# A decode step with paged and windowed attention: state values loaded by place, last pages in two partition halves

## The chip, the cores and the metric

The kernel runs on one core of one Trainium2 chip. The metric is the device time of one execution in microseconds; of several executions the median is given.

## The reference, cut to what matters

One layer of a decoder serves 512 prompt tokens and 8 sequences of 8 sample tokens. Half of the heads use differential attention over 4096 cached positions (paged), the other half a dilated window attention over a state of 2048 positions for each sequence. The part that the change touches is the second half for the samples:

```python
def _dilated_attention_sample(q, k_new, v_new, k_buf, v_buf):
    k_all = concatenate([k_buf, k_new], axis=1)      # 2048 + 8 positions
    v_all = concatenate([v_buf, v_new], axis=1)
    for window, d in ((128, 1), (512, 4), (2048, 16)):
        idx = (w + arange(t))[:, None] - d * arange(window // d + 1)[None, :]
        kg, vg = k_all[:, idx], v_all[:, idx]
        ... softmax over the keys, weighted sum of the values
    # the three branches are combined by their denominators
```

Then follow the output projection, a SwiGLU feed-forward and norms. The state shifted by eight positions is an output too.

## The kernel before

The kernel is written out by hand for each engine, with semaphores. All of the samples' attention runs in a loop of 53 slots `t` with eight steps `i` each, between the pieces of the prompt's work (`pieces(t, i)`). A slot handles a *page set* `q` of one item. An item is a pair of sequences; items 0 to 3 are the paged cache (8 sets each of four pages of 128 positions for each sequence), items 4 to 7 the window state (3 sets each). In all there are 44 sets (`KSLOTS`). Slot `t` scores the keys of set `t` and weighs the values of set `t - 8` (`LAG`). So the state's values are weighed in slots 40 to 51.

A state's 2048 positions are seen as `(p i)` with `i = 16`: 128 places `p`, each of 16 positions. The dilation of 16 makes only positions `4g` to `4g + 3` of every place needed for sets g = 0 and 1, and of the last 32 places positions 8 to 15 (set g = 2, `pages_of(q) == 2`). The latter are the two-page sets 34, 37, 40 and 43, weighed in slots 42, 45, 48 and 51. In each set `h` says which sequence of the pair it is.

Keys go into `k_ring` (eight pages of 128 partitions x 512 floats), are turned in 32x32 blocks by DVE (L2153) into `kt_sb`, and TensorE makes scores from them (L1232). Four-page state keys are loaded two pages at a time. A two-page key load has its source turned by `src.rearrange("p j c -> j p c")` from `[32, 4, 512]` to `[4, 32, 512]`, with the destination `k_ring[:, i, :]`, `[128, 512]`.

Values rotate over three buffers (`ring_of`): `v_ring` up to slot 43, then in turn `k_ring` (44, 47, 50), `v_ring` (45, 48, 51) and `t_ring` (46, 49), which lies over `kt_sb`. All two-page sets are in `v_ring`. `place_values` (L666) issues a load of one page of one `h` (256 KB): row `4j + k` of a buffer gets place or position j of page k, in four blocks b. For a two-page set only partitions 0 to 63 are used, each load goes to 32 of them, 8 KB in each, and sequence h lies in half h of the buffer. `weigh_values` waits for all of a half's pages and multiplies: `turn_probs` has turned the probabilities with four transposes (L1245), ACT copied them to `pt_sb` (L1693), and 32 products (L1270) accumulate in `O`, after which `pv_half[h]` counts up. After an item's last set the new rows are weighed (L1283, `pv_items`).

Up to slot 44 SP issues all values' loads, in `load_values(t, h)`, each with a wait that its buffer is free. From slot 47 on ACT issues the half h = 1, after the copy at L1693 of two slots before. On SP the order at the end is: (41, 6) slot 42 half 0; (42, 0) half 1; (42, 6) and (43, 0) slot 43; (43, 1) slot 44 half 0; (43, 4) slot 46 half 0 and slot 44 half 1; (43, 6) slot 45 half 0; (44, 0) slot 46 half 1 and slot 45 half 1; (44, 6), (45, 6), (46, 6), (47, 6), (48, 6) half 0 of slots 47 to 51. The first weights of the feed-forward stage (`g_raw`, 1 MB each, L737) go out between them. The keys of slot t + 2 and t + 1 are issued in the same loop (L768). After the loop SP waits for `pv_items`, loads `x` again (L714) and enters the feed-forward stage, where TensorE works through to the end.

Of the kernel before, what the change touches and what calls it, by code (L numbers as in the profile page):

```python
# [15 lines left out]
P = 128  # L16
# [82 lines left out]
KSLOTS = sum(QUADS)  # L99
# [12 lines left out]
def pages_of(q):  # L112
    it, g = item_of(q)
    return 2 if it >= 4 and g == 2 else 4
# [14 lines left out]

def col0(it, g):  # L130
    return 512 * g + (0 if it < 4 else WCOLS * ((it - 4) % 3))


def mini0(it):
# [155 lines left out]
def landings():  # L290


    seen, k_lands, v_lands = [[0] * 8 for ring in range(3)], {}, {}
    for q in range(KSLOTS):
        for i in range(8):
            if i % 4 < pages_of(q):
                seen[0][i] += key_load(q, i) == i
                k_lands[q, i] = 16 * seen[0][i]
    for q in range(KSLOTS):
        for i in range(8):  # L300
            if i % 4 < pages_of(q):
                here = seen[ring_of(q + LAG)]
                here[i] += 1
                v_lands[q, i] = 16 * here[i]
    return k_lands, v_lands
# [56 lines left out]
def build(nc, ins, outs):  # L362
    from contextlib import ExitStack
    ctx = ExitStack()
    with ctx:
# [291 lines left out]
        def place_values(queue, q, i, src):  # L657


            h, k = divmod(i, 4)  # L660
            n = pages_of(q)
            if n == 4:
                src = src.rearrange("(b j) c -> j b c", b=4)
            rows, ring = slice(k, 32 * n, n), ring_of(q + LAG)
            dst = (k_ring[rows, 4 * h:4 * h + 4, :], v_ring[rows, h, :, :], t_ring[rows, h, :, :])[ring]
            queue.dma_start(dst, src).then_inc((k_landed, v_landed, t_landed)[ring][i], 16)  # L666

        def state_rows(state, q, i):

# [16 lines left out]
        def _(sp):  # L686
# [61 lines left out]
            def load_page(keys, q, i):  # L748

                it, g = item_of(q)  # L750
                h, k = divmod(i, 4)
                n = pages_of(q)
                if it < 4:
                    if k == 0 and g % 2 == 0:
                        first = (2 * it + h) * NPAGES + 4 * g
                        ids[keys, h] = nc.values_load_multi_w_load_instructions(
                            page_ids[0:1, first:first + 8], engines=[sp.engine], min_val=0, max_val=NPOOL - 1,
                            skip_runtime_bounds_check_because="page_table holds numbers of pages in the pool")[1]
                    src = (ck if keys else cv)[ds(ids[keys, h][4 * (g % 2) + k], 1)].squeeze(0)
                else:  # L760
                    src = state_rows(sk if keys else sv, q, i)
                if keys:
                    if n == 2:
                        src = src.rearrange("p j c -> j p c")
                    elif it >= 4:
                        src = state_pair(sk, q, i)
                    at_first = i - (it >= 4 and n == 4)
                    sp.dma_start(k_ring[:, at_first:i + 1, :].squeeze(1) if at_first == i else k_ring[:, at_first:i + 1, :], src)\  # L768
                        .then_inc(k_landed[i], 16)
                else:  # L770
                    place_values(sp, q, i, src)

            def load_keys(t, i):

# [5 lines left out]

            def load_values(t, h):

                if t == KSLOTS:
                    sp.wait_ge(kt_done, half_end(KSLOTS - 1, h))
                elif t == KSLOTS + 1:
                    sp.wait_ge(pv_half[h], t - LAG - 1)
                elif t == KSLOTS + 2:
                    sp.wait_ge(scored if h else half_scored, KSLOTS)
                elif t > KSLOTS + 2:
                    sp.wait_ge(pv_half[h], t - LAG - 2)  # L790
                elif t > LAG:
                    sp.wait_ge(pv_half[h], t - LAG)
                for k in range(pages_of(t - LAG)):
                    load_page(False, t - LAG, 4 * h + k)

            sp.wait_ge(const_in, 16 * N_CONST)
            for i in range(8):
# [73 lines left out]
            for t in range(SLOTS):  # L871
                for i in range(8):
                    if i < 4:
                        load_keys(t + 1, i + 4)
                    else:
                        load_keys(t + 2, i - 4)
                    for p in pieces(t, i):
                        main(p)
                    if i == 0 and has_v(t - 1) and t < KSLOTS:
                        load_values(t, 1)  # L880
                    if i == 6 and has_v(t) and t + 1 < KSLOTS:
                        load_values(t + 1, 0)
                    if (t, i) == (KSLOTS - 1, 1):
                        load_values(KSLOTS, 0)
                    if (t, i) == (KSLOTS - 1, 4):
                        load_values(KSLOTS + 2, 0)
                        load_values(KSLOTS, 1)
                    if (t, i) == (KSLOTS - 1, 6):
                        load_values(KSLOTS + 1, 0)
                    if (t, i) == (KSLOTS, 0):  # L890
                        load_values(KSLOTS + 2, 1)
                        load_values(KSLOTS + 1, 1)
                    if i == 6 and t >= KSLOTS and has_v(t + 3):
                        load_values(t + 3, 0)
                        if not has_v(t + 4):
                            load_pair(1, 1, 0, w_up, True)
                    if (t, i) == (KSLOTS + 1, 1):
                        sp.wait_ge(e_t, KT)
                        load_pair(0, 0, 0, w_gate, True)
# [109 lines left out]
        def _(pe):  # L1009
# [226 lines left out]
            def turn_probs(t):  # L1236

                it, g = item_of(t - LAG)
                n = pages_of(t - LAG)
                pe.wait_ge(exp_done, EXP_NO[it, 4 * half_of(it, g) + 3] + 1)  # L1240
                if X_NO["p", t]:
                    pe.wait_ge(x_free, X_NO["p", t])
                for k in range(4):
                    c = col0(it, g) + 32 * n * k
                    last = nc.tensor.transpose(X[0:32 * n, k * P:(k + 1) * P], s_sb[:, c:c + 32 * n], ident[:, :])  # L1245
                last.then_inc(x_full, 1)

            def turn_new_probs(t):
# [6 lines left out]
            def weigh_values(t, h):  # L1255

                q = t - LAG
                it, g = item_of(q)
                rows = 32 * pages_of(q)
                pe.wait_ge(x_free, X_NO["p", t] + 1)  # L1260
                if g == 0 and h == 0 and it:
                    pe.wait_ge(o_scaled, it)
                ring = ring_of(t)
                landed = (k_landed, v_landed, t_landed)[ring]
                for k in range(pages_of(q)):
                    pe.wait_ge(landed[4 * h + k], V_LANDS[q, 4 * h + k])
                for b in range(4):
                    values = (k_ring[0:rows, 4 * h + b, :], v_ring[0:rows, h, b, :], t_ring[0:rows, h, b, :])[ring]
                    for f in range(4):
                        last = nc.tensor.matmul(O[32 * f:32 * f + 32, P * h:P * h + P], pt_sb[0:rows, 4 * f + b, :],  # L1270
                                                values[:, f * P:(f + 1) * P],
                                                start=g == 0 and b == 0 and h == 0, stop=False, skip_group_check=True)
                last.then_inc(pv_half[h], 1)

            def weigh_new_values(t):
# [2 lines left out]
                s = it // 4  # L1278
                pe.wait_ge(x_free, X_NO["m", t] + 1)
                pe.wait_ge(y_free, Y_NO["g", 2 * s + 1] + 1)  # L1280
                for h in range(2):
                    for f in range(4):
                        last = nc.tensor.matmul(O[32 * f:32 * f + 32, P * h:P * h + P], ptm[:, 32 * f:32 * f + 32],  # L1283
# [183 lines left out]
        def _(act):  # L1467
# [218 lines left out]
            def evac_probs(t):  # L1686
# [2 lines left out]
                act.wait_ge(x_full, X_NO["p", t] + 1)  # L1689
                if q:  # L1690
                    act.wait_ge(pv_half[1], q)
                r = slice(0, 32 * pages_of(q))
                nc.scalar.activation(pt_sb[r].rearrange("p m (k t) -> p k m t", k=4),  # L1693
                                     X[r].rearrange("p (k m t) -> p k m t", k=4, t=DT), ACT.Copy).then_inc(x_free, 1)
                if t > KSLOTS and has_v(t + 2):
                    for k in range(pages_of(q + 2)):
                        place_values(act, q + 2, 4 + k, state_rows(sv, q + 2, 4 + k))

            def evac_new_probs(t):

# [6 lines left out]
            def exps(it, c):  # L1707
# [7 lines left out]
                else:  # L1715
                    bias = bias4[it % 2][:, k:k + 1]
                    if it >= 4 and half:
                        at0 = col0(it, 2) + 64 * k
                        part = s_sb[:, at0:at0 + 64]
                    else:  # L1720
                        at0, n = col0(it, 4 * half), 4 if it < 4 else 2
# [246 lines left out]
        def _(dve):  # L1968
# [209 lines left out]
            def keep_scores(t):  # L2178
# [7 lines left out]
                    dve.wait_ge(lw_in, 16)  # L2186
                mask = lw[:, P * g:P * g + 32 * n] if it >= 4 else zero.to_broadcast([P, 32 * n])
                for k in range(4):
                    c = col0(it, g) + 32 * n * k
# [437 lines left out]
```

## Time and profile before

| | |
|---|---|
| median of 3 runs | 1122.25 us (1115.1 to 1124.65) |
| the profiled execution's own time | 1113.92 us |
| its span | 1112.1 us |
| TensorE busy | 969.6 us, 87% |
| VectorE busy | 668.9 us, 60% |
| ScalarE busy | 505.7 us, 45% |
| DMA queue of SP, share of 16 engines | 80.3% |
| the stretch of the state's values | from 572 us (first issue) to 696 us (last product) |

Times of the trace are from the span's start. A group of instructions is given with its first start and the time that it took. In brackets stands how long the engine had been idle before it and what ended that. The DMA share is the mean busy share of the core's 16 DMA engines; it can come out a little over 1.

### The profile page before, as it was taken

What the parts mean: (1) busy time and instruction counts of PE and PEld (TensorE: products, weight loads), DVE (VectorE), ACT (ScalarE), POOL (GpSimd) and SP (SyncE); (2) the same over time, 40 slices, a digit from 0 to 9 for tenths busy, and PEclk for the clock granted to TensorE, in tenths of its full rate; (3) what the DMA queues carried; (4) which work ended last, traced back from release to release, by engine and by line L of the source; (5) the groups of instructions that cost most, each with busy time, mean ns of one, the idle gap of its engine ahead of it and who ended that gap; (6) DMA issues with size and microseconds to landing.
All of it is one profiled execution on the core that took longest, in us unless ns stands there. A gap on an engine that the chain in (4) does not pass through costs nothing.

```text
span 1112.1 us, 29337 instructions
## 1 busy us (share of the span) xinstructions
PE 969.6 (87%) x11050; PEld 858.7 (77%) x11050; DVE 668.9 (60%) x1627; ACT 505.7 (45%) x1116; POOL 133.9 (12%) x69
## 2 busy tenths in 40 slices
PE   3989898998887779887889667899999999999995
PEld 3978787777764557676667554699999999999994
DVE  5389645675458887754346445788888888700003
ACT  5654543374125656645234262455555555611123
POOL 1322111111000010002111000000000000133330
PEclk8999999999988999888899787899999999999997
DMA  8699999999999999888979798386768686974632
GB/s 249 248 314 346 320 328 344 358 340 334 317 340 338 337 365 329 301 273 293 327 245 298 221 255 223 123 302 264 301 263 301 263 301 252 325 248 159 228 128 85
DMA packets 174933, 310.98 MB, mean 280 GB/s; under 512 B 13601, under 2 KB 87714, under 8 KB 173282
## 3 DMA queue, kind: packets, MB, share of 16 engines
q1 hardware_dynamic: 172898, 305.24, 80.3%
q10 hardware_dynamic: 1920, 4.20, 1.4%
q8 instruction: 74, 1.21, 0.4%
q14 instruction: 41, 0.34, 0.1%
HBM read 302.30 MB, written 73.92 MB: 338 GB/s over the span
## 4 chain that ended last, share of the span: by engine, by line
PE 32%; issue 30%; DMA 11%; SPq 11%; DVE 7%; ACT 7%; ACTq 0%; POOL 0%; DVEq 0%; POOLq 0%
PE ps L1383 11%; DMA v_ring<-in_cache_v_diff 6%; SPq L666 5%; PE ps L1038 5%; PE ps L1270 4%; PE ps L1232 4%; SPq L768 4%; DVE kt_sb L2153 2%; ACT q_st L1678 2%; PE ps L1189 2%; DMA k_ring<-in_state_v_win 2%; DMA k_ring<-in_cache_k_diff 2%; PE ps L1115 1%; DMA v_ring<-in_state_v_win 1%; ACT s_sb L1723 1%
## 5 line engine op out<-in xcount | busy, mean ns | idle before, releaser
L2153 DVE STREAM_TRANSPOSE kt_sb<-k_ring 128x512 f32<-128x512 f32 x336 | 220.5, 691 | 86.5 <-DMA k_ring<-in_cache_k_diff 37.4
L1270 PE MATMUL ps<-v_ring,pt_sb 128*32 128x128 f32 (+1 forms) x2496 | 98.8, 306 | 62.1 <-DMA v_ring<-in_cache_v_diff 49.3
L1270 PEld LDWEIGHTS ps<-v_ring,pt_sb 128*32 128x32 f32 (+1 forms) x2496 | 75.7, 121 | 78.1 <-issue 67.8
L1038 PE MATMUL ps<-h_hi,w_hi 128*128 128x288 f32 x384 | 124.4, 324 | 1.9 <-DVE h_lo L2006 1.9
L1038 PE MATMUL ps<-h_lo,w_hi 128*128 128x288 f32 x384 | 115.0, 299 | 0.0
L1038 PE MATMUL ps<-h_hi,w_lo 128*128 128x288 f32 x384 | 114.7, 299 | 0.0
L1232 PE MATMUL ps<-kt_sb,q_st 128*32 128x128 f32 (+1 forms) x2816 | 97.0, 281 | 10.2 <-DVE q_st L2163 4.6
L989 POOL TENSOR_TENSOR c_lo<-c_raw,c_hi 128x1408 fp32r<-128x1408 f32 x14 | 46.6, 3332 | 440.2 <-ACT c_hi L1781 440.2
L1232 PEld LDWEIGHTS ps<-kt_sb,q_st 128*32 128x32 f32 x2816 | 72.9, 114 | 28.2 <-issue 19.9
L1038 PEld LDWEIGHTS ps<-h_hi,w_hi 128*128 128x128 f32 x384 | 74.0, 193 | 16.1 <-issue 13.8
L949 POOL TENSOR_TENSOR w_lo<-w_raw,w_hi 128x1024 fp32r<-128x1024 f32 x24 | 57.3, 2390 | 229.5 <-ACT w_hi L1492 229.5
L1693 ACT ACTIVATE pt_sb<-ps 128x512 f32<-128x512 f32 (+1 forms) x44 | 26.2, 594 | 129.2 <-PE ps L1245 129.2
L1320 PE MATMUL ps<-t_h,s_h 128*128 128x288 f32 x264 | 77.9, 295 | 1.2 <-ACT u L1774 1.2
L1320 PE MATMUL ps<-t_l,s_h 128*128 128x288 f32 x264 | 77.9, 295 | 0.0
L1320 PE MATMUL ps<-t_h,s_l 128*128 128x288 f32 x264 | 77.7, 294 | 0.0
L2444 DVE TENSOR_TENSOR x<-x,ps 128x512 f32 (+1 forms) x8 | 5.5, 689 | 119.5 <-PE ps L1396 119.5
L2292 DVE TENSOR_TENSOR s_l<-s_t,s_h 128x512 fp32r<-128x512 f32 x88 | 58.8, 689 | 28.4 <-ACT s_h L1745 18.1
L1383 PE MATMUL ps<-a_hi,c_hi 128*128 128x288 f32 x352 | 75.4, 296 | 0.2 <-POOL c_lo L989 0.2
L1383 PE MATMUL ps<-a_lo,c_hi 128*128 128x288 f32 x352 | 75.3, 295 | 0.0
L1383 PE MATMUL ps<-a_hi,c_lo 128*128 128x288 f32 x352 | 74.9, 294 | 0.0
L1038 PEld LDWEIGHTS ps<-h_lo,w_hi 128*128 128x128 f32 x384 | 74.3, 194 | 0.0
L1038 PEld LDWEIGHTS ps<-h_hi,w_lo 128*128 128x128 f32 x384 | 73.9, 192 | 0.0
(236 smaller groups left out, 2289.4 us busy)
## 6 DMA issues: line engine op xcount, KB each, us to landing
k_ring<-in_cache_k_diff SPq DMA_DIRECT2D x256, 256.0 KB, 5.5
v_ring<-in_cache_v_diff SPq DMA_DIRECT2D x256, 256.0 KB, 5.5
out_k_win_sample<-in_state_k_win SPq DMA_DIRECT2D x32, 1020.0 KB, 8.3
out_v_win_sample<-in_state_v_win SPq DMA_DIRECT2D x32, 1020.0 KB, 8.5
k_ring<-in_state_k_win SPq DMA_DIRECT2D x32, 512.0 KB, 7.7
w_raw<-in_w_in SPq DMA_DIRECT2D x24, 512.0 KB, 6.3
g_raw<-in_w_gate SPq DMA_DIRECT2D x11, 1024.0 KB, 5.2
g_raw<-in_w_up SPq DMA_DIRECT2D x11, 1024.0 KB, 5.2
```

Of the source, the lines that this page charges most:

```text
L666: queue.dma_start(dst, src).then_inc((k_landed, v_landed, t_landed)[ring][i], 16)
L768: sp.dma_start(k_ring[:, at_first:i + 1, :].squeeze(1) if at_first == i else k_ring[:, at_first:i + 1, :], src)\
L949: nc.gpsimd.tensor_tensor(w_lo[:, n % 3, :], w_raw[:, n % 3, :], w_hi[:, n % 2, :].bitcast(F32), ALU.subtract).then_inc(w_lo_done, 1)
L989: nc.gpsimd.tensor_tensor(c_lo[j][:, 0:width], c_raw[:, j, 0:width], c_hi[j][:, 0:width].bitcast(F32), ALU.subtract).then_inc(w_lo_done, 1)
L1038: last = nc.tensor.matmul(M[c][:, 0:HALF], wt, act[:, k, c * HALF:(c + 1) * HALF], start=k == 0 and at_first, stop=k == KT - 1 and act is ...
L1232: last = nc.tensor.matmul(S[32 * f:32 * f + 32, c0:c0 + 32 * n], q_st[:, h, f, r, :], kt_sb[:, 4 * h:4 * h + n, c:c + 32], start=r % 2 == ...
L1270: last = nc.tensor.matmul(O[32 * f:32 * f + 32, P * h:P * h + P], pt_sb[0:rows, 4 * f + b, :], values[:, f * P:(f + 1) * P], start=g == 0 ...
L1320: last = nc.tensor.matmul(ps[:, bank, 0:HALF], wt[:, k, :], act[:, k, :], start=j in (0, 1, 3) and k == 0 and at_first, stop=k == 3 and wt ...
L1383: last = nc.tensor.matmul(main_ps[:, 2 * bank + c, 0:HALF], wt[j][:, w], a_lo[:, pair, block, :] if low else a_hi[pair][:, block, :], star ...
L1693: nc.scalar.activation(pt_sb[r].rearrange("p m (k t) -> p k m t", k=4), X[r].rearrange("p (k m t) -> p k m t", k=4, t=DT), ACT.Copy).then_ ...
L2153: V.transpose(kt_sb[:, i, :], k_ring[:, i, :]).then_inc(kt_done, 1)
L2292: V.tensor_tensor(dst[:, :, :], src, high[:, :, :].bitcast(F32), ALU.subtract).then_inc(form_low, 1)
```

## The change

Values of the state are now loaded by `place_state`. For a four-page set a load fills one block b (all 128 partitions, 2 KB in each) from 32 places, and in each place from four positions that lie side by side (8 KB). For a two-page set one load fetches 4 of the 8 positions of both sequences (512 KB), to every second partition of all 128, 8 KB in each; sequence h is now in partitions 64h to 64h + 63, and the set fills only half `it % 2` of `v_ring`. There are two such loads for a set instead of four. The scores of such a set lie in another order (`part0`), are turned with two transposes instead of four and copied with two copies of 64 partitions. TensorE waits block by block in four-page state sets, waits for its own products of h = 0 before those of h = 1 in two-page sets, and for all of them before the new rows of items 4 to 7. Both loads for slot 45 go out at (43, 6); those for slot 48 at (44, 0) and for slot 51 at (45, 6), earlier than before. Slot 43's loads both wait for slot 42's second half.

```diff
+def part0(q, k):
+    it, g = item_of(q)
+    return col0(it, g) + (P * k if pages_of(q) == 4 else 64 * (2 * (k % 2) + k // 2))
@@ landings
-            if i % 4 < pages_of(q):
+            if pages_of(q) == 4 or i - 4 * (item_of(q)[0] % 2) in (0, 1):
@@ place_values: only for n == 4 now, and
+        def place_state(queue, q, h, x):
+            it, g = item_of(q)
+            b, ring = 2 * (it - 4) + h, ring_of(q + LAG)
+            if pages_of(q) == 4:
+                dst = (k_ring[:, 4 * h + x, :], v_ring[:, h, x, :], t_ring[:, h, x, :])[ring]
+                queue.dma_start(dst, sv[b, 32 * x:32 * x + 32, 4 * g:4 * g + 4, :])\
+                    .then_inc((k_landed, v_landed, t_landed)[ring][4 * h + x], 16)
+            else:
+                src = sv[b:b + 2, 96:P, 8 + 4 * x:12 + 4 * x, :].rearrange("h j b c -> h j (b c)")
+                queue.dma_start(v_ring[x:P:2, it % 2, :, :].rearrange("p b c -> p (b c)"), src).then_inc(v_landed[4 * (it % 2) + x], 16)
@@ load_values
+                q = t - LAG
+                if pages_of(q) == 2:
+                    if h == 0:
+                        half = item_of(q)[0] % 2
+                        q0 = {FIRST[4] + 2: q - 1, FIRST[5] + 2: q - 2, FIRST[6] + 2: q - 5, FIRST[7] + 2: q - 6}[q]
+                        sp.wait_ge(pv_half[half], q0 + 1)
+                        for x in range(2):
+                            place_state(sp, q, h, x)
+                    return
-                    sp.wait_ge(pv_half[h], t - LAG)
+                    sp.wait_ge(pv_half[1 if pages_of(q - 1) == 2 else h], q)
@@ SP's loop
                         load_values(KSLOTS + 2, 1)
-                        load_values(KSLOTS + 1, 1)
+                        load_values(KSLOTS + 4, 0)
+                    if (t, i) == (KSLOTS + 1, 6):
+                        load_values(KSLOTS + 7, 0)
                     if i == 6 and t >= KSLOTS and has_v(t + 3):
-                        load_values(t + 3, 0)
+                        if pages_of(t + 3 - LAG) == 4:
+                            load_values(t + 3, 0)
@@ turn_probs
-                for k in range(4):
-                    c = col0(it, g) + 32 * n * k
-                    last = nc.tensor.transpose(X[0:32 * n, k * P:(k + 1) * P], s_sb[:, c:c + 32 * n], ident[:, :])
+                for k in range(n):
+                    c = col0(it, g) + P * k
+                    last = nc.tensor.transpose(X[:, k * P:(k + 1) * P], s_sb[:, c:c + P], ident[:, :])
@@ weigh_values
+                rows, at = (slice(0, P), h) if n == 4 else (slice(64 * h, 64 * h + 64), it % 2)
+                if n == 2 and h == 1:
+                    pe.wait_ge(pv_half[0], q + 1)
+                by_place = it >= 4 and n == 4
                 for b in range(4):
+                    if by_place:
+                        pe.wait_ge(landed[4 * h + b], V_LANDS[q, 4 * h + b])
@@ weigh_new_values
+                if it >= 4:
+                    pe.wait_ge(pv_half[1], FIRST[it] + QUADS[it])
@@ evac_probs
+                    for h in range(2):
+                        r = slice(64 * h, 64 * h + 64)
+                        last = nc.scalar.activation(into[r, 2 * h:2 * h + 2],
+                                                    X[r, 0:2 * P].rearrange("p (k m t) -> p k m t", k=2, t=DT), ACT.Copy)
-                    for k in range(pages_of(q + 2)):
-                        place_values(act, q + 2, 4 + k, state_rows(sv, q + 2, 4 + k))
+                    if pages_of(q + 2) == 4:
+                        for b in range(4):
+                            place_state(act, q + 2, 1, b)
```

## Rows read from the trace of the kernel before

**Rows 1.** The page: busy time of TensorE, and the DMA queue of SP.
```profile
PE 969.6 (87%) x11050; PEld 858.7 (77%) x11050; DVE 668.9 (60%) x1627; ACT 505.7 (45%) x1116; POOL 133.9 (12%) x69
...
q1 hardware_dynamic: 172898, 305.24, 80.3%
```

**Rows 2.** Windows: length, busy times (instructions) of each engine, clock, DMA share, GB/s.
```profile
594.00:595.00 1.00, 1.00 (x23) 0.76 (x13) 0.21 (x1) 1.00 (x2) 0.28 (x1) 1.00 0.96 391
...
600.00:602.00 2.00, 1.29 (x19) 0.95 (x21) 1.97 (x6) 1.91 (x8) 0.00 (x0) 1.00 1.03 382
...
635.00:640.00 5.00, 0.78 (x12) 0.42 (x4) 1.64 (x11) 3.53 (x12) 0.00 (x0) 0.98 1.03 361
640.00:645.00 5.00, 0.20 (x4) 0.20 (x8) 1.60 (x3) 4.94 (x16) 0.00 (x0) 0.50 1.04 224
...
660.00:670.00 10.00, 5.11 (x112) 3.90 (x104) 5.04 (x8) 5.39 (x8) 0.00 (x0) 1.00 1.05 225
...
680.00:690.00 10.00, 6.74 (x139) 5.00 (x137) 3.65 (x7) 1.55 (x2) 0.00 (x0) 0.88 1.01 208
```

**Rows 3.** TensorE in order of time: start, us, line, operation, count, idle before.
```profile
572.04 0.60 PE L1245 MATMUL ps<-ident,s_sb 128*128 128x128 f32 x4
...
620.52 1.93 PE L1270 MATMUL ps<-v_ring,pt_sb 64*32 64x128 f32 x32 [4.82 <-DMA v_ring<-in_state_v_win]
...
622.73 1.94 PE L1232 MATMUL ps<-kt_sb,q_st 128*32 128x128 f32 x32
625.04 1.93 PE L1270 MATMUL ps<-v_ring,pt_sb 64*32 64x128 f32 x32 [0.37 <-DMA v_ring<-in_state_v_win]
...
633.50 0.65 PE L1232 MATMUL ps<-kt_sb,q_st 128*32 128x64 f32 x32
...
644.80 3.64 PE L1270 MATMUL ps<-k_ring,pt_sb 128*32 128x128 f32 x64 [9.02 <-ACT pt_sb L1693]
...
670.14 1.66 PE L1270 MATMUL ps<-v_ring,pt_sb 64*32 64x128 f32 x32 [3.56 <-DMA v_ring<-in_state_v_win]
...
687.42 1.86 PE L1270 MATMUL ps<-k_ring,pt_sb 128*32 128x128 f32 x32 [2.44 <-DMA k_ring<-in_state_v_win]
...
693.16 1.93 PE L1270 MATMUL ps<-v_ring,pt_sb 64*32 64x128 f32 x32
694.87 1.08 PE L1283 MATMUL ps<-v_s,ptm 64*32 64x128 f32 x16
```

**Rows 4.** The chain that ended last: start, us, what.
```profile
612.62 12.28 DMA v_ring<-in_state_v_win
...
668.57 18.71 DMA k_ring<-in_state_v_win
```

**Rows 5.** Windows as in rows 2, of two gaps.
```profile
617.00:620.00 3.00, 0.00 (x0) 0.00 (x0) 1.51 (x6) 0.00 (x0) 0.00 (x0) 0.88 0.25 83
...
575.00:577.00 2.00, 0.00 (x0) 0.00 (x0) 1.20 (x6) 0.00 (x0) 0.00 (x0) 1.00 0.30 101
```

**Rows 6.** SP in order of time: start, us of issuing, line, what, count.
```profile
601.56 3.88 SPq L768 DMA_DIRECT2D k_ring<-in_state_k_win  x4
607.29 1.16 SPq L666 DMA_DIRECT2D v_ring<-in_state_v_win  x2
611.47 0.58 SPq L768 DMA_DIRECT2D k_ring<-in_state_k_win  x1
612.10 1.13 SPq L666 DMA_DIRECT2D v_ring<-in_state_v_win  x2
613.27 0.58 SPq L768 DMA_DIRECT2D k_ring<-in_state_k_win  x1
...
696.01 0.47 SPq L714 DMA_DIRECT2D x<-in_x_sample  x1
```

**Rows 7.** Single durations: ACT's copies, and ACT's issues of loads (ns min/median/max).
```profile
L1693 ACT ACTIVATE pt_sb<-ps x44: 573/597/603, 132.7 to 690.3; 128x512 f32<-128x512 f32 x40, 64x512 f32<-64x512 f32 x4
...
L666 ACTq DMA_DIRECT2D v_ring<-in_state_v_win x4: 509/568/612, 657.9 to 676.5; - x4
```

More of the change, by code:

```diff
@@ L660, in place_values @@
             h, k = divmod(i, 4)
[L661 to L664, printed above, removed]
+            rows, ring = slice(k, P, 4), ring_of(q + LAG)
             dst = (k_ring[rows, 4 * h:4 * h + 4, :], v_ring[rows, h, :, :], t_ring[rows, h, :, :])[ring]
-            queue.dma_start(dst, src).then_inc((k_landed, v_landed, t_landed)[ring][i], 16)
+            queue.dma_start(dst, src.rearrange("(b j) c -> j b c", b=4))\
+                .then_inc((k_landed, v_landed, t_landed)[ring][i], 16)
+        def place_state(queue, q, h, x):
[8 more added lines that the diff above has]
+                queue.dma_start(v_ring[x:P:2, it % 2, :, :].rearrange("p b c -> p (b c)"), src).then_inc(v_landed[4 * (it % 2) + x], 16)
         def state_rows(state, q, i):
@@ L759, in load_page @@
                     src = (ck if keys else cv)[ds(ids[keys, h][4 * (g % 2) + k], 1)].squeeze(0)
-                else:
-                    src = state_rows(sk if keys else sv, q, i)
+                elif keys:
+                    src = state_rows(sk, q, i)
                 if keys:
@@ L769, in load_page @@
                         .then_inc(k_landed[i], 16)
+                elif it < 4:
+                    place_values(sp, q, i, src)
                 else:
-                    place_values(sp, q, i, src)
+                    place_state(sp, q, h, k)
             def load_keys(t, i):
@@ L781, in load_values @@
             def load_values(t, h):
+                q = t - LAG
[7 more added lines that the diff above has]
+                    return
                 if t == KSLOTS:
                     sp.wait_ge(kt_done, half_end(KSLOTS - 1, h))
-                elif t == KSLOTS + 1:
-                    sp.wait_ge(pv_half[h], t - LAG - 1)
                 elif t == KSLOTS + 2:
@@ L789, in load_values @@
                 elif t > KSLOTS + 2:
-                    sp.wait_ge(pv_half[h], t - LAG - 2)
+                    sp.wait_ge(pv_half[h], q - 2)
                 elif t > LAG:
-                    sp.wait_ge(pv_half[h], t - LAG)
-                for k in range(pages_of(t - LAG)):
-                    load_page(False, t - LAG, 4 * h + k)
+                    sp.wait_ge(pv_half[1 if pages_of(q - 1) == 2 else h], q)
+                for k in range(4):
+                    load_page(False, q, 4 * h + k)
             sp.wait_ge(const_in, 16 * N_CONST)
@@ L1258, in weigh_values @@
                 it, g = item_of(q)
-                rows = 32 * pages_of(q)
+                n = pages_of(q)
+                rows, at = (slice(0, P), h) if n == 4 else (slice(64 * h, 64 * h + 64), it % 2)
                 pe.wait_ge(x_free, X_NO["p", t] + 1)
@@ L1264, in weigh_values @@
                 landed = (k_landed, v_landed, t_landed)[ring]
-                for k in range(pages_of(q)):
-                    pe.wait_ge(landed[4 * h + k], V_LANDS[q, 4 * h + k])
+                if n == 2 and h == 1:
+                    pe.wait_ge(pv_half[0], q + 1)
+                by_place = it >= 4 and n == 4
+                if not by_place:
+                    for k in range(n):
+                        pe.wait_ge(landed[4 * at + k], V_LANDS[q, 4 * at + k])
                 for b in range(4):
-                    values = (k_ring[0:rows, 4 * h + b, :], v_ring[0:rows, h, b, :], t_ring[0:rows, h, b, :])[ring]
+                    if by_place:
+                        pe.wait_ge(landed[4 * h + b], V_LANDS[q, 4 * h + b])
+                    values = (k_ring[rows, 4 * at + b, :], v_ring[rows, at, b, :], t_ring[rows, at, b, :])[ring]
                     for f in range(4):
-                        last = nc.tensor.matmul(O[32 * f:32 * f + 32, P * h:P * h + P], pt_sb[0:rows, 4 * f + b, :],
+                        last = nc.tensor.matmul(O[32 * f:32 * f + 32, P * h:P * h + P], pt_sb[rows, 4 * f + b, :],
                                                 values[:, f * P:(f + 1) * P],
@@ L1691, in evac_probs @@
                     act.wait_ge(pv_half[1], q)
-                r = slice(0, 32 * pages_of(q))
-                nc.scalar.activation(pt_sb[r].rearrange("p m (k t) -> p k m t", k=4),
-                                     X[r].rearrange("p (k m t) -> p k m t", k=4, t=DT), ACT.Copy).then_inc(x_free, 1)
+                into = pt_sb[:].rearrange("p m (k t) -> p k m t", k=4)
+                if pages_of(q) == 4:
+                    last = nc.scalar.activation(into, X.rearrange("p (k m t) -> p k m t", k=4, t=DT), ACT.Copy)
+                else:
+                    for h in range(2):
+                        r = slice(64 * h, 64 * h + 64)
+                        last = nc.scalar.activation(into[r, 2 * h:2 * h + 2],
+                                                    X[r, 0:2 * P].rearrange("p (k m t) -> p k m t", k=2, t=DT), ACT.Copy)
+                last.then_inc(x_free, 1)
                 if t > KSLOTS and has_v(t + 2):
-                    for k in range(pages_of(q + 2)):
-                        place_values(act, q + 2, 4 + k, state_rows(sv, q + 2, 4 + k))
+                    if pages_of(q + 2) == 4:
+                        for b in range(4):
+                            place_state(act, q + 2, 1, b)
             def evac_new_probs(t):
@@ L1717, in exps @@
                     if it >= 4 and half:
-                        at0 = col0(it, 2) + 64 * k
+                        at0 = part0(FIRST[it] + 2, k)
                         part = s_sb[:, at0:at0 + 64]
@@ L2188, in keep_scores @@
                 for k in range(4):
-                    c = col0(it, g) + 32 * n * k
+                    c = part0(t, k)
                     last = V.tensor_tensor_reduce(out=s_sb[:, c:c + 32 * n].rearrange("p (j x) -> p j x", x=n),
```

## The prediction

> **What bounds the kernel now.** I read the page first [rows 1]: TensorE is busy for 87% of the span and the DMA queue for 80%, averages over stages with different limits. The diff touches only the values of the dilated items: slots 40 to 51, with their loads from 572 us on and their last products at 695 us. So I read that stretch by windows. At 600:602, with keys of 4 KB pieces, the DMA share is 1.03 and 382 GB/s move; at 635:640 it is 1.03 with 361 GB/s. In 640:645, 660:670 and 680:690 the share is just as full but only 224, 225 and 208 GB/s move [rows 2]. From 630 to 690 the transfers bound the stage, and part of them moves at little over half rate. TensorE's side agrees: it starts slot 48 at 670.14 after 3.56 us of waiting for `v_ring`, slot 50's second half at 687.42 after 2.44 us for `k_ring`, and ends the last values product at 693.16 + 1.93 = 695.1 and the new rows at 695.95 [rows 3]. The chain of waits goes through a transfer of 18.71 us there, and through one of 12.28 us before slot 42's second half [rows 4].
>
> The row that decides my forecast is 617:620: DMA share 0.25, 83 GB/s, and 575:577 is like it with 0.30 and 101 [rows 5]. A quarter of the DMA engines' time is 4 of 16 engines, while TensorE sat idle for 4.82 us before 620.52 waiting for values [rows 3]. What was outstanding then: the 256 KB loads of two-page keys, issued from 601.56 to 613.27, and the values of slot 42 behind them [rows 6]. A two-page key load has the source `[4, 32, 512]` (leading dimension 4, by `p j c -> j p c`) and the destination `[128, 512]`; 4 divides both. The stage's other loads have leading dimensions of 32 or 128, and windows that hold only them show a full share. So, as I read it, a transfer is laid out over as many engines as its leading dimensions share as a divisor, and 256 KB of keys occupy four engines for 64 KB each instead of sixteen for 16 KB. The 12.28 us transfer agrees: 256 KB of values, spread over all engines, waited on the four that still had keys in their queues.
>
> The Trainium skill (DMA: Bandwidth & Descriptors, section "Why a DMA increments its semaphore by 16 and not by 1") states this: the engine count k is the largest number up to 16 that divides the slowest dimension (other than 1) of both access patterns, and the hardware queue takes the lowest-numbered k. By that rule the key loads get 4, and the trace agrees with 0.25. By the same rule the new value loads, `[2, 32, 2048]` into `[64, 2048]`, get 2 engines; if every load got 16, the sum below would be that of the second rival.
>
> **Rates of one engine.** Row 617:620 gives 83/(16 x 0.25) = 20.8 GB/s, row 600:602 382/(16 x 1.03) = 23.2, row 594:595 391/(16 x 0.96) = 25.4 [rows 2, 5]. I take 23 for pieces of 2 KB. The new two-page pieces are 8 KB, longer than any of those, so I take the highest, 25.4, and keep 20.8 as the other end.
>
> **The change part by part.**
>
> *Two-page values (slots 42, 45, 48, 51).* Sixteen loads of 256 KB become eight of 512 KB, with h = 2 as the leading source dimension. By the pattern of the keys each runs on two engines: 256 KB / 25.4 = 10.3 us, and the two loads of a slot, one behind the other on the same engines, 20.6 us (25.2 at 20.8 GB/s). Every later load from SP also has a share in these two engines and waits behind them, as slot 42's values did behind the keys. So I add up the queue of one such engine; the others idle.
>
> 1. Slot 42. The loads are issued at 607.29 as now [rows 6]. Engine 0 is through with earlier keys at about 617: the values that landed for 620.5 were 32 KB on it, about 2.8 us at the half rate of 640:645 (224/16.6 = 13.5 GB/s gives 2.4). 617 + 20.6 = 637.6, so the products start 17.1 us later than 620.52. The keys issued at 611.47 and 613.27 follow, 2 x 64 KB / 23 = 5.7 us, to 643.3.
> 2. Slot 43's values now both wait for slot 42's second half (`pv_half[1]`). That is 637.6 + 1.93 + 1.94 + 1.93 = 643.4 with the key products between [rows 3]. Eight issues of 0.58 us [rows 6] hold SP to 648.3, then `k_ring`'s four to about 651. Queued behind this wait on SP are only loads of slots 44 to 46; they move with it. The engine has caught up by 651.
> 3. From 651 engine 0 is never empty: 12 loads of slots 44 and 46 (16 KB each, 8.5 us), slot 45 (20.6), four of slot 46 (2.85), slot 48 (20.6), eight of slot 47 (5.7), the first `g_raw` (64 KB, 2.85), slot 51 (20.6), slots 49 and 50 (2 x 5.7). The sum is 93.1 us, to 744.1. The exponentials of the last item, 634.1 to 644.8 on the page of before [rows 3], move to some 653 to 664 and lie beside slot 45's load.
> 4. After its last load for slot 50 the kernel now takes 695.95 - 687.42 = 8.5 us [rows 3]. 744.1 + 8.5 = 752.6 against 695.95: **56.7 us later**. What follows (`load_x(4)` at 696.01, the feed-forward stage) hangs on `pv_items` and moves as a whole.
>
> *Four-page values by place.* The same 64 loads of 256 KB with pieces of 2 KB, leading dimensions 32 and 128, so 16 engines as before. Sources become 8 KB runs. No row shows an 8 KB run cut in 2 KB pieces; from below, 64 x 256 KB at 361 instead of 382 GB/s are 46.5 and 43.9 us, so at most 2.6 us gained, and as much lost on the other side. I take nothing. Waiting for one block b at a time lets 8 of 32 products start early: three quarters of a half's 1.86 us, 1.4 us, where a four-page half waited for its load (687.42 [rows 3]): 1.4 us, and hidden once another load is late.
>
> *Small parts.* Two transposes for four (the four take 0.60 us [rows 3]) save 0.3 us x 4. One copy of 64x512 (0.573 to 0.603 us [rows 7]) becomes two of 64x256: between 0 and 0.6 us more, x 4. The drains before the second half and before the new rows are eight: below, nothing, when the products are through; above, 0.37 us each, as long as TensorE idled for a semaphore before 625.04 [rows 3], 3.0 us together (all of TensorE's queue stands behind them). ACT loses four issues of 0.51 to 0.61 us [rows 7]. Scores kept in another order cost DVE the same instructions. All lie beside the late loads; together within 3 us, taken as nothing. Without that cover they would be seen as up to 3 us.
>
> Sum: 1112.1 + 56.7 = 1168.8 us of span, 1113.9 + 56.7 = 1170.6 in the profiled execution's own time. The median of before, 1122.25, lies 8.3 us over that execution, so by the median it is 1179. The runs shown scatter over 9.5 us; I take 1174.
>
> **Rivals.** About 1%, 11 us, is what a measurement of this kernel can tell from no change.
>
> *Second: the loads spread over all 16 engines* (the source is cut along its 32 rows, or its two halves are laid out over sixteen). Against it: the share of 0.25 under the key loads. For it: that is one pattern with 4, none with 2. The last pages would then reach both halves of the partitions, where today 32 partitions of the lower 64 take them; the rows of 208 to 225 GB/s fall where these loads run. The Trainium skill (SBUF — State Buffer, section "Door 1: The DMA port swizzle (why `[64,N]` ≈ `[32,N]`)") has partitions 0 to 63 reach only 8 of 16 ports; the rows of half rate agree. Price by rows: 4.19 MB at 361 instead of 224 GB/s, 18.7 - 11.6 = 7 us, with slots 48 and 51 asked for earlier, the 3.56 us before 670.14 gone and up to 1.4 us of block waits: 7 to 12 us less, **1112** by the median. This comes out ahead of before, from the point where one load uses at least eight engines: then the pair costs 5 us, about what it costs now.
>
> *Third: two engines, but early issue hides it.* Slot 48 is asked for before slot 47 and slot 51 before slots 49 and 50. For it: each has tens of us until its use. Against it: the queue of the engine is one behind the other, and all that follows on SP's queue needs it, so time asked for early is no time saved. Were it so, only slot 42's 17 us and part of 45's remained beside the present waits of 7 us: about 1140 at the best, and within 1% only if both were covered too.
>
> *Fourth: the new waits for the own products* (drains) as the only cost: +3.0 us, 1125, no change that can be told. It needs the loads to cost what they cost now.
>
> **How the numbers follow.** Two engines with the full queue 0.82; two engines partly hidden (1140 to 1150) 0.05; sixteen engines 0.09, of which half by more than 1% faster; no change for other reasons 0.04. Hence faster 0.05, same 0.08, slower 0.87. Range: at 20.8 GB/s the four pairs cost 4 x 4.6 = 18 us more, 1174 + 18 = 1192, with a few us of crowding at most 1198. Downward, one of the four pairs hidden (20.6) gives 1153; I take 1150.
>
> **What would show each step.** DMA share of about 0.13 with some 50 GB/s in windows between 620 and 740 says two engines; a full share with over 300 GB/s says sixteen. Transfers of `v_ring` from the state should take 20 us and more to land, and loads of `k_ring` and `t_ring` issued behind them as long. TensorE's wait before the products of slot 42 should grow from 4.8 to about 22 us, and it should wait again in slots 45, 46, 47 and 49. The feed-forward stage should be the same length, started 57 us later. If that stage starts before 700, or if the wait before slot 42 is under 5 us, the engine count was wrong; if it starts between 715 and 735, the rate or the serial queue was.

## The result

The changed kernel takes 1180.45 us (median of 6 runs, 1173.97 to 1186.57), the kernel before 1116.94 us (now also 6 runs, 1111.86 to 1124.65). The ratio is 1.056, 95% interval 1.050 to 1.061: about 63 us slower. The profiled execution took 1178.52 us, its span is 1176.7 us. Forecast were 1174 us, range 1150 to 1198.

The page of the kernel after, its header, its busy times and the queue of SP:

```profile
span 1176.7 us, 29301 instructions
...
PE 980.8 (83%) x11042; PEld 862.7 (73%) x11042; DVE 668.8 (57%) x1627; ACT 506.7 (43%) x1120; POOL 134.0 (11%) x69
...
q1 hardware_dynamic: 172850, 306.29, 75.1%
```

The same bytes take 64.6 us more of span, and the DMA engines are *less* busy than before [rows 1]: 75.1% instead of 80.3%. TensorE is busy for 11.2 us more with eight matmul instructions fewer; the rest is waiting.

Windows of the kernel after (length, busy us of each engine, clock, DMA share, GB/s):

```profile
630.00:635.00 5.00, 0.00 (x0) 0.00 (x0) 0.00 (x0) 0.00 (x0) 0.00 (x0) 0.50 0.13 52
635.00:640.00 5.00, 1.74 (x32) 1.50 (x32) 0.00 (x0) 0.00 (x0) 0.00 (x0) 0.50 0.14 52
...
650.00:660.00 10.00, 4.96 (x93) 2.83 (x85) 3.18 (x22) 5.82 (x15) 0.00 (x0) 0.67 1.01 359
...
680.00:690.00 10.00, 3.09 (x39) 2.09 (x39) 0.00 (x0) 0.77 (x3) 0.00 (x0) 0.50 0.28 94
...
710.00:715.00 5.00, 0.00 (x0) 0.00 (x0) 0.00 (x0) 0.00 (x0) 0.00 (x0) 0.50 0.13 50
```

A share of 0.13 is 2 of 16 engines, at 52/2 = 26 GB/s each, while in the first and the last of these windows every other engine of the core does nothing. At 650:660, before slot 45's two-engine loads (issued at 657.77) come up in the queue, ordinary loads move 359 GB/s, like the row at 635:640 of before [rows 2]. In what follows a load that runs on fewer than 16 engines is called *confined*.

TensorE of the kernel after, in order of time (start, us, what, idle before it and its releaser), at the same places as [rows 3]:

```profile
638.26 1.93 PE L1312 MATMUL ps<-v_ring,pt_sb 64*32 64x128 f32 x32 [18.40 <-DMA v_ring<-in_state_v_win]
...
642.34 1.93 PE L1312 MATMUL ps<-v_ring,pt_sb 64*32 64x128 f32 x32
644.45 1.08 PE L1329 MATMUL ps<-v_s,ptm 64*32 64x128 f32 x16 [0.18 <-PE ps L1312]
...
686.91 1.93 PE L1312 MATMUL ps<-v_ring,pt_sb 64*32 64x128 f32 x32 [17.95 <-DMA v_ring<-in_state_v_win]
...
696.61 1.93 PE L1312 MATMUL ps<-t_ring,pt_sb 128*32 128x128 f32 x32 [0.69 <-ACT pt_sb L1740]
...
715.04 0.65 PE L1312 MATMUL ps<-k_ring,pt_sb 128*32 128x128 f32 x8 [12.67 <-DMA k_ring<-in_state_v_win]
...
747.61 2.55 PE L1312 MATMUL ps<-t_ring,pt_sb 128*32 128x128 f32 x32 [13.44 <-DMA t_ring<-in_state_v_win]
...
753.64 1.96 PE L1312 MATMUL ps<-k_ring,pt_sb 128*32 128x128 f32 x64 [0.69 <-ACT pt_sb L1740]
...
756.82 1.08 PE L1312 MATMUL ps<-v_ring,pt_sb 64*32 64x128 f32 x32 [0.86 <-ACT pt_sb L1744]
...
759.31 1.08 PE L1329 MATMUL ps<-v_s,ptm 64*32 64x128 f32 x16 [0.17 <-PE ps L1312]
```

The values' stage ends at 759.31 + 1.08 = 760.4 instead of 695.95, 64.4 us later; what follows is of the same length. Four stalls of 12.7 to 18.4 us make up most of it, in slots 42, 45, 47 and 49: 62.5 us together, where before waits 4.82 us for its values in slot 42, 0.66 in slot 45 and not at all in the other two. Only the first two are in slots that the confined loads serve. Slots 47 and 49 wait for ordinary loads into `k_ring` and `t_ring` that stood behind confined ones. The chain shows the same (start, us, what):

```profile
612.20 25.92 DMA v_ring<-in_state_v_win
...
658.37 28.40 DMA v_ring<-in_state_v_win
...
715.81 31.67 DMA t_ring<-in_state_v_win
```

### The profile page after: what moved, and what is told of

It reads as the page before. It is cut to its first block, busy times and chain, and to the rows that moved or that the text cites. A ratio compares the mean times of both kernels' runs of the same rounds, so it can differ in the third digit from the quotient of the medians.

```text
span 1176.7 us, 29301 instructions
## 1 busy us (share of the span) xinstructions
PE 980.8 (83%) x11042; PEld 862.7 (73%) x11042; DVE 668.8 (57%) x1627; ACT 506.7 (43%) x1120; POOL 134.0 (11%) x69
## 3 DMA queue, kind: packets, MB, share of 16 engines
q1 hardware_dynamic: 172850, 306.29, 75.1%
## 4 chain that ended last, share of the span: by engine, by line
PE 31%; issue 28%; DMA 16%; SPq 13%; DVE 7%; ACT 4%; POOL 0%; ACTq 0%; DVEq 0%; POOLq 0%
PE ps L1429 10%; PE ps L1071 6%; SPq L670 6%; DMA v_ring<-in_state_v_win 5%; DMA v_ring<-in_cache_v_diff 5%; PE ps L1312 4%; SPq L787 3%; PE ps L1265 3%; DMA t_ring<-in_state_v_win 3%; DMA k_ring<-in_cache_k_diff 3%; DVE kt_sb L2206 2%; PE ps L1222 2%; SPq L685 1%; ACT q_st L1724 1%; SPq L681 1%
## 5 line engine op out<-in xcount | busy, mean ns | idle before, releaser
L1740 ACT ACTIVATE pt_sb<-ps 128x512 f32<-128x512 f32 x40 | 23.8, 596 | 136.5 <-PE ps L1278 136.5
```

The source lines that it names most:

```text
L1740: last = nc.scalar.activation(into, X.rearrange("p (k m t) -> p k m t", k=4, t=DT), ACT.Copy)
```

## The experiments

Each kernel ran beside runs of the kernel before on the same chip; ratios are to those runs, and where a time of before is given, it is their median.

**1. The same change on all engines (e1_all16).**

```diff
-                src = sv[b:b + 2, 96:P, 8 + 4 * x:12 + 4 * x, :].rearrange("h j b c -> h j (b c)")
-                queue.dma_start(v_ring[x:P:2, it % 2, :, :]..., src).then_inc(v_landed[4 * (it % 2) + x], 16)
+                for s in range(2):
+                    src = sv[b + s, 96:P, 8 + 4 * x:12 + 4 * x, :].rearrange("j b c -> j (b c)")
+                    queue.dma_start(v_ring[64 * s + x:64 * s + 64:2, it % 2, :, :]..., src).then_inc(v_landed[4 * (it % 2) + x], 16)
```

> The changed kernel, with each two-page load of values cut into one load for each sequence: source [32, 2048], leading dimension 32, the same partitions, waits and places in the order. Theory (engine count by the leading dimension): these loads run on 16 engines, the windows of DMA share 0.13 and 52 GB/s vanish, slot 42's values land within some 12 us instead of 26, and the whole 60 us goes: 1105 to 1122 us, ratio to before 0.99 to 1.005. Rival (the new waits, the moved issues or the layout by place cost the time): stays above 1150.

Measured: 1114.59 us (10 runs) against 1115.77 us, ratio 1.0003, interval 0.997 to 1.0035. All of the loss is gone, with the layout, the early issues and every new wait kept. The 25.92 us transfer of slot 42 is now this row of the chain:

```profile
611.54 10.35 DMA v_ring<-in_state_v_win
```

This undoes the leading dimension of 2, but also the merging of loads that brought it (16 loads of 256 KB again instead of 8 of 512 KB); experiment 2 tells the two apart. The rest of the change is worth nothing that this measurement can tell.

**2. The leading dimension alone, in the kernel before (e_lead2).** The four 256 KB loads of a two-page set keep their bytes, pieces, partitions, waits and places in the order.

```diff
+            if n == 2:
+                dst = dst.rearrange("p b c -> p (b c)")
+                src = src.rearrange("(j a) b c -> a j (b c)", a=2)
             queue.dma_start(dst, src)
```

> The kernel before, with the rows of each two-page values load taken in the order of (j a), a = 2 leading: source [2, 16, 2048], 32 partitions as before, all else unchanged (a set's last rows so lie in other partitions than their probabilities, and that part of the output is not the reference's). Theory: two engines for each of the four 256 KB loads of a slot, 5.2 us each, the same 20.6 us of a slot's queue as in the changed kernel: 1165 to 1185 us with DMA share near 0.13 in gaps. Rival (something else in the change costs the time, or the first dimension does not set the engine count): within 1% of before, 1106 to 1128.

Measured: 1174.42 us (2 runs), ratio 1.053, interval 1.046 to 1.060. A kernel with nothing of the change but a leading 2 loses 59 of the 63 us, with loads of 256 KB. In its trace SP's load of `x` after the loop starts at 758.31, 62.3 us later than at 696.01 in before [rows 6]. Its windows have the same signature:

```profile
620.00:625.00 5.00, 0.00 (x0) 0.00 (x0) 1.50 (x7) 0.33 (x1) 0.00 (x0) 0.86 0.13 54
...
640.00:645.00 5.00, 2.33 (x45) 2.36 (x48) 0.00 (x0) 0.00 (x0) 0.00 (x0) 0.50 0.13 49
```

**3. The dose (e_lead4).** The same edit with `a=4`.

> The kernel before, with the rows of each two-page values load in the order of (j a), a = 4 leading: source [4, 8, 2048] (that part of the output is not the reference's, as with a = 2). Theory (k is that dimension): four engines, 64 KB each, 2.6 us a load and 10.3 us a slot at full port rate; half the extra time of a = 2 or somewhat less, 1125 to 1147 us, and a DMA share near 0.25 in the gaps. Rival (any small leading dimension falls back to the same slow form): as a = 2, 1165 or more.

Measured: 1137.64 us (2 runs), ratio 1.020, interval 1.015 to 1.025. That is 23 us, 0.39 of what a leading 2 costs. By the forecast's terms a slot's queue is 10.3 us where a spread one is some 5 and a confined one 20.6, so (10.3 - 5)/(20.6 - 5) = 0.34 of it follows; the expectation said half or somewhat less. The gap windows sit at a quarter:

```profile
620.00:625.00 5.00, 1.49 (x31) 1.09 (x24) 2.70 (x8) 1.07 (x2) 0.00 (x0) 0.77 0.25 99
```

Shares of 0.13, 0.25 and 1.0 for leading dimensions of 2, 4 and 32 are 2, 4 and 16 engines. With these sizes no run tells "the largest common divisor up to 16" from "the smaller of the two dimensions, at most 16".

**4. Is one late slot enough, or does each add its share? (e_only42, e_only51).** In the changed kernel only slot 42's, or only slot 51's, loads are cut as in experiment 1 (its branch with the condition `q == FIRST[4] + 2` or `q == FIRST[7] + 2`).

> The changed kernel with slot 42's loads alone cut for each sequence; slots 45, 48 and 51 stay on two engines. Theory (one serial queue, each slot's loads cost 20.6 us in it where spread ones cost some 5): about a quarter of the loss is gone, 1160 to 1168 us. Rival (the first late slot is what costs, later ones are hidden): 1120 to 1140.

> The changed kernel with slot 51's loads alone cut for each sequence; slots 42, 45 and 48 stay on two engines. Theory (one serial queue): a quarter of the loss is gone too, 1160 to 1168 us, though these loads are issued early. Rival (loads issued early are hidden): no change, 1175 to 1185.

Measured, against 1114.61 us: 1165.22 us for slot 42 (2 runs, ratio 1.045, interval 1.040 to 1.050) and 1166.20 us for slot 51 (2 runs, 1.046, 1.040 to 1.051). Over their own runs of before they lose 50.6 and 51.6 us, where the changed kernel loses 63.5: each gives back 12 to 13 us, a fifth of the loss. The traces say the same: `x` is loaded after the loop at 748.13 and 749.06, 12.3 and 11.4 us before the 760.44 of the kernel after. The forecast term was 20.6 - 5 = 15.6 us; with two runs each, an uncertainty of some 5 us on each side includes it. Cutting slot 42's loads brings its own wait back to what before has:

```profile
624.65 1.93 PE L1317 MATMUL ps<-v_ring,pt_sb 64*32 64x128 f32 x32 [5.22 <-DMA v_ring<-in_state_v_win]
```

Slots 45, 47 and 49 go on waiting there (16.13, 16.37 and 13.46 us). In e_only51 the waits of slots 42, 45 and 47 stay (18.87, 18.64 and 14.60 us for the first of its blocks), and the 13.44 us of slot 49 are gone, whose loads stood behind slot 51's in the queue. The third rival is out: slot 51's loads are asked for tens of us before their use (issued from 697.68, used at 756.82 in the kernel after), and cost about as much as slot 42's, whose use waits at once.

**5. The layout by place alone (e_place).** The kernel before, with four-page state sets loaded by `place_state` and awaited block by block; two-page sets as before.

```diff
-                    place_values(sp, q, i, src)
+                elif it >= 4 and n == 4:
+                    place_state(sp, q, h, k)
...
                 for b in range(4):
+                    if by_place:
+                        pe.wait_ge(landed[4 * h + b], V_LANDS[q, 4 * h + b])
```

> The kernel before, with only the four-page state values loaded by place and awaited block by block; the two-page sets as before. Theory: same number of loads, bytes, pieces and engines, so within 0.5% of before (1112 to 1121 us); block waits are worth at most 1.4 us. Rival (the layout by place is part of the loss, since the changed kernel was already 4 us late at slot 42's first issue): 3 to 6 us slower, 1120 to 1123.

Measured: 1112.92 us (12 runs) against 1115.77, ratio 0.9966, interval 0.9938 to 0.9993. It is no loss; at most it is a gain of a few us (3.8 by the ratio, 0.8 to 6.9 by its interval), where I allowed 1.4 us for block waits. Whether the rest comes from the 8 KB runs or from scatter is not settled.

**6. The keys' engine count (e_keys16).** The kernel before has its own confined loads: two-page keys with a leading dimension of 4.

```diff
-                        src = src.rearrange("p j c -> j p c")
+                        for j in range(4):
+                            sp.dma_start(k_ring[32 * j:32 * j + 32, i, :], src[:, j, :]).then_inc(k_landed[i], 16)
+                        return
```

> The kernel before, with each two-page load of state keys (source leading dimension 4) cut into four loads of 32 rows, 64 KB each, to the same places. Theory: keys go over 16 engines, the gap at 617 to 620 us with share 0.25 vanishes, slot 42's values land some 5 us earlier, and SP has 48 issues more, of 0.6 us each, spread over four items: 1105 to 1117 us. Rival (the keys' 4 engines were a coincidence of an empty queue): the share of 0.25 stays, and time is the same or up to 10 us slower by the issues.

Measured: 1099.72 us (4 runs), ratio 0.985, interval 0.980 to 0.990: 16 us faster than before, in spite of 48 issues more, and faster than the 1105 to 1117 that I expected. In the trace nearly all of the gain is there by slot 42 (first row, TensorE as in [rows 3]; second row, a window as in [rows 5]):

```profile
607.72 1.08 PE L1272 MATMUL ps<-v_ring,pt_sb 64*32 64x128 f32 x32 [0.68 <-ACT pt_sb L1695]
...
617.00:620.00 3.00, 3.00 (x78) 2.38 (x73) 1.11 (x10) 0.40 (x1) 0.00 (x0) 0.58 1.01 377
```

The products that began at 620.52 after 4.82 us of waiting [rows 3] begin at 607.72 after none for a transfer. That is 12.8 us earlier, 4.1 us by the shorter wait and 8.7 us because TensorE came to slot 42 that much sooner. My expectation counted only the first; what gave the second was not followed. The gap at 617 to 620 us [rows 5] is gone, as the second row shows; since the kernel is further on by then, it shows other loads than the row of before.

**7. Both repairs (e_both16).** Experiments 1 and 6 together.

> The changed kernel with both repairs: two-page values loaded for one sequence at a time (leading dimension 32) and two-page keys in four loads of 32 rows. Theory: no load is confined any more; the keys' gain of about 16 us comes on top of a changed kernel that without the confinement equals before: 1093 to 1102 us. Rival (the split keys' issues on SP collide with the values' loads, or the two gains are the same gap counted twice): 1105 to 1115.

Measured: 1092.28 us (6 runs) against 1114.61, ratio 0.980, interval 0.977 to 0.983. This beats both kernels: 22 us under before, 88 under the change as it was made. It lies just below the 1093 to 1102 expected, and far from the rival's 1105 to 1115.

**8. What the half rate comes from (e_ports).** In the kernel before, the two-page values go to every fourth of all 128 partitions.

```diff
-            rows, ring = slice(k, 32 * n, n), ring_of(q + LAG)
+            rows, ring = slice(k, P, 4), ring_of(q + LAG)
```

> The kernel before, with each two-page load of values going to every fourth of all 128 partitions instead of every second of the lower 64 (32 partitions of 8 KB in both; the products read the rows they read before, so that part of the output is not the reference's). Theory (the half rate of 208 to 225 GB/s at a full DMA share comes from writing to the lower 64 partitions alone): the windows of full share move 300 GB/s and more where the 8 KB pieces run, and the DMA-bound stretch gets 5 to 10 us shorter: 1104 to 1110 us where before is 1115. Rival (the half rate comes from pieces of 8 KB, or from memory): rate and time stay, 1112 to 1118.

Measured: 1110.29 us (12 runs) against 1114.07, ratio 0.9966, interval 0.9935 to 0.9996. The rate is as the theory has it; the first of these windows of e_ports stands against 224 GB/s at a share of 1.04 in [rows 2]:

```profile
640.00:645.00 5.00, 0.00 (x0) 0.00 (x0) 1.60 (x3) 4.94 (x10) 0.00 (x0) 0.50 1.03 379
...
660.00:665.00 5.00, 3.89 (x77) 3.06 (x77) 3.48 (x7) 2.44 (x5) 0.00 (x0) 1.00 0.90 311
665.00:670.00 5.00, 2.51 (x68) 2.05 (x68) 1.19 (x1) 3.11 (x5) 0.00 (x0) 1.00 0.88 273
```

The time is not: 1110.29 lies just outside the theory's 1104 to 1110, and by the ratio it is 4 us (0.4 to 7.2 by the interval) instead of 5 to 10. The last two rows show that with the half rate gone the share falls to 0.9: the transfers are no longer what the stage always waits for. TensorE's waits in the stretch (in all, times, longest) say what is instead:

```profile
PE ps L1270 <- ACT pt_sb L1693: 16.9, 9, 8.8
PE ps L1270 <- DMA v_ring<-in_state_v_win: 4.5, 2, 2.3
```

The same view of before:

```profile
PE ps L1270 <- ACT pt_sb L1693: 13.0, 7, 9.0
PE ps L1270 <- DMA v_ring<-in_state_v_win: 9.4, 4, 4.8
...
PE ps L1270 <- DMA k_ring<-in_state_v_win: 3.3, 2, 2.4
```

That is 8.2 us less for transfers, 3.9 us more for ACT's copies, 4 us in sum. The Trainium skill (SBUF — State Buffer, section "Door 1: The DMA port swizzle (why `[64,N]` ≈ `[32,N]`)") gives the lower 64 partitions 8 of 16 ports; the two rates, 224 and 379 GB/s at a share of 1.04 and 1.03, agree with it.

## Why the prediction was right, point by point

- **Two engines.** Shown. Share 0.13 and 52 GB/s where I had named 0.13 and 50; undone by experiment 1, made alone by 2, graded by 3.
- **25.4 GB/s for pieces of 8 KB.** 52 GB/s over two engines is 26. The value taken was right; the bound of 20.8 played no part.
- **Step 1, slot 42.** 637.6 forecast, 638.26 measured. The loads were issued at 611.64 instead of 607.29, but engine 0 still had keys before them: the products' start less 20.6 us gives 617.7, as against my 617. The wait before the products is 18.4 us, not the "about 22" that I named last, since TensorE too came there later, at 619.86 instead of 615.70. I take that for the scatter of single executions: slot 42's first load is issued at 608.73 in e1_all16, which has the whole change but the confinement, and at 613.58 in e_ports, where nothing is changed ahead of it. That the engine was free at the forecast time although everything was issued 4.35 us later is not explained; to that extent the 637.6 came out by luck.
- **Step 2.** SP went on at 644.33 (643.4 forecast), and `k_ring`'s loads were out at 652.6 (651). (Eight issues of 0.58 us from 643.4 end at 648.0, not 648.3; nothing hangs on it.)
- **Step 3, a serial queue.** Its mechanism is shown by experiment 4. Its term, 15.6 us more for a slot, was measured as 12 to 13. I had listed waits in slots 45, 46, 47 and 49. Slot 46 had none (0.69 us for ACT at 696.61). Its first half was issued before slot 45's loads, and its second needed only 2.85 us of the engine behind them, while TensorE had slot 45 to do.
- **Steps 3 and 4, where the sum fell short.** It ended the stage 56.7 us later, measured are 64.4. At 747.61 TensorE still waited for slot 49, where the sum had the engine through with slot 50's loads at 744.1: 3.5 us, of which 1.6 were there at the end of step 2. From then to the end it takes 760.4 - 747.6 = 12.8 us, not the 8.5 that I took from before, because slots 49, 50 and 51 were all still to be done when slot 49's loads landed, and the 8.5 us began at slot 50's second half. But the two places in the queue are not the same. On SP, slot 50's first half was issued after slot 49's (from 727.08), and its 4 x 16 KB at 23 GB/s take 2.85 us of the engine, so that the engine was through with slot 50 at about 750.3 (an estimate; the DMA share falls from 0.91 at 745:748 to 0.19 at 748:750, 0.11 at 750:753 and 0.06 at 753:756). Compared at that place, the queue was some 6 us longer than the sum had it, and the tail behind it some 1.6 us. Most of the error is therefore in steps 2 and 3, the queue of one engine; 1.6 of the 6 us were there at the end of step 2, and what made up the rest is open. Part of the order was also wrong: ACT's loads for slot 47 (issued from 668.13 to 670.74) went beside slot 45's confined ones, not after slot 48's; that moves the wait of slot 45, not the end.
- **TensorE's clock, left out.** These are the waits of the kernel after, of TensorE in the stretch (engine, line, releaser, us in total, times, longest):

```profile
PE ps L1312 <- DMA v_ring<-in_state_v_win: 37.0, 5, 18.4
PE ps L1312 <- DMA k_ring<-in_state_v_win: 13.4, 3, 12.7
PE ps L1312 <- DMA t_ring<-in_state_v_win: 13.4, 1, 13.4
```

  Together 63.8 us; the same view of before has 9.4 for `v_ring` and 3.3 for `k_ring`. That is 51 us more, and TensorE's 11.2 us of additional busy time bring it to 62, near the 64.4. The busy time grew because after each stall the granted clock is 0.50, the level of 1.2 GHz: the 32 products of slot 46's first half take 1.93 us at 696.61, where before took 1.08 (at 658.51), and 32 products like slot 42's take 1.08 us again at 756.82, where the clock was up. It lies partly beside the queue (without it TensorE would have waited longer for the transfers), so it costs less than 11 us.
- **The second rival** fell with its condition. It would not have paid as much as I said either: with all loads on 16 engines the change equals before (experiment 1). There a load for one sequence still reaches only one half of the partitions, and one window of its trace (645:650) still has 225 GB/s at a share of 1.02. The full rate in both halves is worth 4 us (experiment 8), not 7 to 12. Both together, one load over both halves on 16 engines, was not run.
- **The fourth rival, the drains.** They cost 0.17 to 0.18 us each before the new rows (the rows at 644.45 and 759.31), below my upper bound of 0.37, and experiment 1, which keeps them, is as fast as before.
- **1174 against 1180.45.** By the profiled executions the sum gave 1170.6 against 1178.52, 7.9 us short. Added to the median of before as I had it (1122.25, three runs) it gave 1179, near the measured time only because that median was 5 us too high (1116.94 with six runs). From 1179 I went down to 1174 for the scatter of the runs; that 1116.94 + 56.7 = 1173.6 is nearly the same is chance. The range was wide enough for the queue's missing microseconds; the mechanism was right, its length was not.

## What to carry to other kernels

Before a DMA is merged with another, look at the outermost dimension of its source and its destination: two sequences as a leading 2 put half a megabyte on two of sixteen engines, and every later load waits behind it. A DMA share of k/16 while somebody waits for a transfer is the sign to look for, and it was in the profile of before: the loads of keys with a leading 4, worth 16 us (experiment 6). The share alone is not enough: e1_all16 has a window of 0.14 at 625:630 too, but with 34 GB/s where two engines at work move some 50, and with TensorE busy. A confined load is not hidden by asking for it early, because the time is in the queue of the engines, not in its own latency.

## What had not been expected

A full queue holds its issuer, as I read it. Issues of the kernel after on SP (ns min/median/max in the first row, then start and us):

```profile
L685 SPq DMA_DIRECT2D v_ring<-in_state_v_win x8: 525/1592/15491, 611.6 to 713.2; - x8
...
667.43 16.31 SPq L685 DMA_DIRECT2D v_ring<-in_state_v_win  x2
683.79 9.93 SPq L681 DMA_DIRECT2D k_ring<-in_state_v_win  x4
...
697.68 18.09 SPq L685 DMA_DIRECT2D v_ring<-in_state_v_win  x2
```

One issue took 15.49 us where the kernel before has at most 1.67 us for a load of the state's values into `v_ring`. I had counted 0.58 us each. The chain of waits goes through these issues (12.31 and 2.55 us of SP just before the transfer at 715.81). I think that they cost nothing of their own here, since the two engines were busy all the while, but no run tells that apart. It means in any case that the time from issue to landing understates such a load's delay: slot 47's first half was issued at 683.79, after SP had stood for 16 us in the issues before it. A load that needed none of the confined engines' time would still have stood behind SP; that was not tested.
